# Expert tokens and results through row tables in DRAM, and expert weights in slices of 1024 columns

## The chip, the cores and the metric

The kernel runs on one core of one Trainium2 chip. The metric is the device time of one execution in microseconds, the median of several runs.
## The reference

Two decoder layers over 256 tokens of width 1024: an RG-LRU block and a dense SwiGLU, then forgetting attention and a mixture of eight SwiGLU experts of which each token uses two. The change is about the mixture:

```python
def _moe(xn, router, w_gu, w_down):
    logits = (xn @ router).astype(jnp.float32)
    top_v, top_i = lax.top_k(logits, TOP_K)              # TOP_K = 2
    w = jax.nn.softmax(top_v, axis=-1)
    gates = jnp.sum(w[..., None] * jax.nn.one_hot(top_i, N_EXPERTS, dtype=jnp.float32), axis=-2)
    y = jnp.zeros_like(xn)
    for e in range(N_EXPERTS):                           # 8 experts, D_EXP = 3584
        y = y + gates[..., e:e + 1].astype(xn.dtype) * _swiglu(xn, w_gu[e], w_down[e])
    return y
...
hn = _rmsnorm(x, norm_g[l, 1]); x = x + _moe(hn, ...);  return _rmsnorm(x, final_norm_g)
```

## The kernel before

All weights are float32 and stream once from DRAM in units of 1 MB (128 partitions x 2048 columns), 403 of them: 65 for the layers up to attention, 8 x 42 for the experts, and two that nobody uses. SyncE loads unit u into one of six slots of `raw` (L209) as soon as VectorE is done with unit u - 6 (`lo_done`). ScalarE copies it, rounded to float32r, into one of three slots of `w_hi` (L331, `split_hi`); it waits there until TensorE has used unit u - 3 (`unit_used`). VectorE puts the rest, raw - w_hi, into `w_lo` (L570, `split_lo`). TensorE multiplies in three parts (`mm3`, L959 to L961): hi x lo, lo x hi, hi x hi. ScalarE and VectorE run two units ahead of TensorE (LEAD = 2): with unit k on TensorE they split unit k + 2.

A loop over `jobs` passes of one expert each (eight, or sixteen where an expert has more than 128 tokens) holds for all engines. One pass is 42 units, cut in seven chunks of 512 hidden columns: four units of gate and up weights (`expert_in`, 512 columns each, so runs of 2 KB in DRAM), and two of down weights (`expert_out`). The token tiles `act_hi`, `act_lo` are the stationary operand of gate and up. After a chunk: silu of the gate on ScalarE (L544), product with up on VectorE (L925, `hid`), four transposes on TensorE (`hidden_T`, L1216), `hid_hi` on ScalarE (L548) and `hid_lo` on VectorE (L931). These stand ahead of the split of their place k in ScalarE's and VectorE's order. The hidden tiles are the stationary operand of `expert_out`.

The tokens of an expert come by TensorE: `gather` (L1179, L1180) multiplies the token rows with a 0/1 matrix `sel` that VectorE builds from the ranks of the router, 32 matmuls, between the second last and the last down unit of chunk 5. The results go back in the same way one pass later: at k = 0 ScalarE and VectorE split the result by the slots' gates (`y_hi` L528, `y_lo` L897), TensorE transposes the gated selection and multiplies (`scatter`, L1190, L1191, eight matmuls), VectorE adds to `x` (L905). After the loop comes the last scatter, then the final norm and the store.

What stands in what order is written out by hand for each engine; no planner is in it. Ahead of the loop come the router's small steps on VectorE, POOL's subtraction for the token rows' low part (L319), and filler matmuls (`keep_warm`, L994) that end with 14 just before the first expert.

## Time and profile before

| | |
|---|---|
| median of three runs (1528.9 to 1529.28) | 1529.24 us |
| span of the profiled execution | 1527.8 us |
| TensorE busy, share of the span | 1478.3 us, 97% |
| VectorE, ScalarE, POOL busy | 1177.1, 978.8, 20.4 us |
| DMA moved | 426.91 MB, mean 279 GB/s |
| DMA rate in the slices of the expert loop (38 us each) | 305 to 374 GB/s |
| matmuls of `expert_in` (each of L959 to L961) | 896 |
| expert loop, first to last matmul | about 503 to 1512.6 us |

A row of the order of time begins with the start and the duration in us; several instructions of one kind in a row are merged, with their number behind x; the idle time of the engine before it and what ended it stand in brackets. The duration of a matmul is longer than the distance to the next one, since they overlap: the distance of two starts is what one costs. "DMA share" is the mean busy share of the 16 DMA engines.

### The profile page before, as it was taken

The numbers are of one execution on the slowest core, as the hardware profiler recorded it, in microseconds if no ns is written. First come the engines' busy times: TensorE is split into PE (matmuls) and PEld (weight loads), VectorE is DVE, ScalarE is ACT, GpSimd is POOL, SyncE is SP. The second block draws the span as 40 slices with busy tenths as digits, with TensorE's granted clock in tenths as the row PEclk, the third lists the DMA queues.
The fourth block names the chain that finished last, engine by engine and source line by source line (L and its number), as shares of the span: only waits on it lengthen the run. The fifth ranks groups of instructions, "written<-read, shape, count | busy, mean of one in ns | idle before, by whom it ended". The sixth has DMA issues, their size and how long they took to land.

```text
span 1527.8 us, 20924 instructions
## 1 busy us (share of the span) xinstructions
PE 1478.3 (97%) x7697; PEld 1244.9 (81%) x7697; DVE 1177.1 (77%) x1030; ACT 978.8 (64%) x859; POOL 20.4 (1%) x30
## 2 busy tenths in 40 slices
PE   6979999999999999999999999999999999999996
PEld 5969999989777888788788878878878887887885
DVE  5765544484456888889898888888889888888887
ACT  4835344354343777777777777777776777777774
POOL 0200000000001000000000000000000000000000
PEclk8999999999999999999999999999999999999998
DMA  9444555645114699999999989989999999998993
GB/s 307 138 165 160 172 191 177 188 130 191 59 56 151 224 362 369 321 358 362 319 356 362 374 309 364 366 310 362 368 322 356 357 349 334 359 374 305 368 363 118
DMA packets 206372, 426.91 MB, mean 279 GB/s; under 512 B 8728, under 2 KB 51840, under 8 KB 206336
## 3 DMA queue, kind: packets, MB, share of 16 engines
q1 hardware_dynamic: 203552, 424.75, 78.4%
q10 hardware_dynamic: 2640, 1.15, 0.3%
q0 software_dynamic: 144, 0.52, 0.1%
q8 instruction: 23, 0.38, 0.1%
q14 instruction: 13, 0.11, 0.0%
HBM read 425.35 MB, written 1.05 MB: 279 GB/s over the span
## 4 chain that ended last, share of the span: by engine, by line
PE 91%; DVE 3%; ACT 3%; issue 2%; ACTq 1%; DMA 0%; POOL 0%; DVEq 0%; POOLq 0%; SPq 0%
PE bank L959 28%; PE bank L961 27%; PE bank L960 27%; PE bank L1216 2%; ACT w_hi L331 1%; DVE w_lo L570 1%; PE bank L1117 1%; PE bank L1180 1%; PE bank L1179 1%; ACT y_hi L528 1%; PE bank L1190 1%; PE bank L1191 1%; PE bank L1115 1%; PE bank L1140 0%; PE bank L1130 0%
## 5 line engine op out<-in xcount | busy, mean ns | idle before, releaser
L570 DVE TENSOR_TENSOR w_lo<-raw,w_hi 128x2048 fp32r<-128x2048 f32 x403 | 917.9, 2292 | 255.6 <-ACT w_hi L331 254.8
L331 ACT ACTIVATE w_hi<-raw 128x2048 fp32r<-128x2048 f32 x403 | 771.5, 1918 | 261.0 <-PE bank L961 251.0
L959 PE MATMUL bank<-w_hi,act_lo 128*128 128x512 f32 x896 | 355.1, 396 | 9.6 <-DVE w_lo L570 9.6
L961 PE MATMUL bank<-w_hi,act_hi 128*128 128x512 f32 x896 | 349.5, 390 | 0.0
L960 PE MATMUL bank<-w_lo,act_hi 128*128 128x512 f32 x896 | 349.2, 390 | 0.0
L959 PE MATMUL bank<-w_hi,hid_lo 128*128 128x512 f32 x536 | 213.3, 398 | 0.0
L960 PE MATMUL bank<-w_lo,hid_hi 128*128 128x512 f32 x536 | 212.4, 396 | 0.0
L961 PE MATMUL bank<-w_hi,hid_hi 128*128 128x512 f32 x536 | 212.3, 396 | 0.0
L959 PEld LDWEIGHTS bank<-w_hi,act_lo 128*128 128x128 f32 x896 | 168.3, 188 | 47.7 <-DVE w_lo L570 14.2
L961 PEld LDWEIGHTS bank<-w_hi,act_hi 128*128 128x128 f32 x896 | 168.2, 188 | 36.2
L960 PEld LDWEIGHTS bank<-w_lo,act_hi 128*128 128x128 f32 x896 | 168.5, 188 | 33.4
L959 PE MATMUL bank<-act_hi,w_lo 128*128 128x256 f32 x608 | 174.7, 287 | 11.2 <-DVE act_lo L587 11.2
L961 PE MATMUL bank<-act_hi,w_hi 128*128 128x256 f32 x608 | 173.2, 285 | 0.0
L960 PE MATMUL bank<-act_lo,w_hi 128*128 128x256 f32 x608 | 173.2, 285 | 0.0
L959 PEld LDWEIGHTS bank<-act_hi,w_lo 128*128 128x128 f32 x608 | 117.9, 194 | 13.5 <-issue 12.9
L961 PEld LDWEIGHTS bank<-w_hi,hid_hi 128*128 128x128 f32 x536 | 100.9, 188 | 24.4
L959 PEld LDWEIGHTS bank<-w_hi,hid_lo 128*128 128x128 f32 x536 | 101.0, 188 | 23.2
L960 PEld LDWEIGHTS bank<-w_lo,hid_hi 128*128 128x128 f32 x536 | 100.9, 188 | 23.2
L960 PEld LDWEIGHTS bank<-act_lo,w_hi 128*128 128x128 f32 x608 | 117.8, 194 | 0.5
L961 PEld LDWEIGHTS bank<-act_hi,w_hi 128*128 128x128 f32 x608 | 117.8, 194 | 0.0
L544 ACT ACTIVATE silu<-bank 128x512 f32<-128x512 f32 x56 | 33.5, 599 | 42.3 <-PE bank L961 42.2
L959 PE MATMUL bank<-w_hi,alt_lo 128*128 128x512 f32 x96 | 38.7, 403 | 6.2 <-DVE alt_lo L655 6.2
(226 smaller groups left out, 1158.9 us busy)
## 6 DMA issues: line engine op xcount, KB each, us to landing
raw<-in_moe_w_gu SPq DMA_DIRECT2D x226, 1024.0 KB, 6.6
raw<-in_moe_w_down SPq DMA_DIRECT2D x112, 1024.0 KB, 6.1
raw<-in_mlp_w_gu SPq DMA_DIRECT2D x22, 1024.0 KB, 5.0
raw<-in_mlp_w_down SPq DMA_DIRECT2D x11, 1024.0 KB, 5.0
raw<-in_lru_w_in SPq DMA_DIRECT2D x8, 1024.0 KB, 12.5
raw<-in_w_kvf SPq DMA_DIRECT2D x8, 1024.0 KB, 5.4
raw<-in_fox_w_qg SPq DMA_DIRECT2D x8, 1024.0 KB, 5.3
raw<-in_lru_w_out SPq DMA_DIRECT2D x4, 1024.0 KB, 5.2
```

What stands on the lines that cost most here:

```text
L331: a.activation(w_hi[:, u % SPL, :], raw[:, u % RAW, :], ACT.Copy).then_inc(hi_done, 1)
L528: a.activation(y_hi[:, HALF * half:HALF * half + HALF], bank[half][:], ACT.Copy, scale=gslot[:, 0:1]).then_inc(yhi_done, 1)
L544: a.activation(silu[:], bank[2][:], ACT.Silu).then_inc(e_silu, 1)
L570: v.tensor_tensor(w_lo[:, u % SPL, :], raw[:, u % RAW, :], w_hi[:, u % SPL, :].bitcast(f32), ALU.subtract).then_inc(lo_done, 1)
L959: t_.matmul(dst, l_lo, r_hi, start=start, stop=False)
L960: t_.matmul(dst, l_hi, r_lo, start=False, stop=False)
L961: return t_.matmul(dst, l_hi, r_hi, start=False, stop=stop)
L1115: t_.matmul(dst, c_sel[:, i % 2, queries], c_neg[:, keys], start=True, stop=False)
L1117: last = t_.matmul(dst, q_T[rows_h, hp, queries], k_T[rows_h, hp, keys], start=False, stop=True)
L1179: t_.matmul(dst, src_lo[:, w], sel[:, t, :], start=(t == 0), stop=False)
L1180: last = t_.matmul(dst, src_hi[:, w], sel[:, t, :], start=False, stop=(t == NT - 1))
L1216: last = t_.transpose(bank[4 + c % 2][:, n * P:(n + 1) * P], hid[:, n * P:(n + 1) * P], ident[:])
```

## The change

Tokens. The kernel gets two tables of 17 x 128 rows in DRAM, `tok_rows` and `y_rows`. POOL fills both with zeros, 17 DMAs of 0.5 MB each, behind its second and its third norm step. For each token two row numbers are worked out (`row_i`), one for each of its experts. POOL scales the normed token rows (`xs_g`) and writes them with four indirect DMAs to their rows. Expert 0 still takes its tokens by `gather`; each later one loads its 128 rows of `tok_rows` into `tok` in the pass before (an ACT DMA at k = 10), and TensorE transposes them (`tokens_T`, eight transposes after unit 37) into the token tiles. ScalarE doesn't enter the loop before all four writes have landed.

Results. There is no scatter. At the end of a pass ScalarE copies the 128 x 1024 result from PSUM to `y_sb` and issues its store to `y_rows`. After the loop POOL waits for all stores and issues four indirect gathers; VectorE multiplies each with the tokens' gates and adds it to `x`.

Weights. Gate and up are loaded in slices of 1024 columns (three pairs) and one of 512: units of [128, 2, 1024], runs of 4 KB. A pass is G0 U0 G1 D0 ... in the order of the tables `G_AT`, `U_AT`, `D_AT`. silu, `hid` and `hid_lo` work on 1024 columns, four times a pass instead of seven on 512; `hidden_T` stands after units 11, 23, 33 and 39. `expert_in` works on two PSUM banks in turn with the same stationary tile.

Place. A tile of 32 bytes (`pad_to_64_bytes`) is put ahead of the tiles that share one region. `hid_hi` starts at byte 174304 of a partition before and at 178560 afterwards, that is at 32 and at 0 past a multiple of 64; `hid_lo` likewise. `act_hi`, `act_lo`, `alt_hi`, `alt_lo` and the weight tiles start at a multiple of 64 in both.

```diff
-CH = D_EXP // 512
-JU = 6 * CH
+JU = 42
+NPAIR = 4
+WIDE = 1024
+G_AT, U_AT, D_AT = (0, 8, 20, 32), (4, 12, 24, 34), (16, 28, 36, 40)
+GU_UNITS, D_UNITS = (4, 4, 4, 2), (4, 4, 4, 2)
+T_AFTER = (11, 23, 33, 39)
+TOK_AFTER = 37
+ROWS = 17 * P
...
+        sb("pad_to_64_bytes", [P, PAD])
...
@@ sync @@
+                            kt, width = (2, WIDE) if n == 4 else (4, 512)
+                            lo = part + WIDE * p
+                            return e_gu[e][:, kt * (k - at):kt * (k - at) + kt, lo:lo + width], width
...
@@ gpsimd @@
             norm_scale(1)
+            pool.wait_ge(zeros_ready, 1)
+            for b in range(ROWS // P):
+                pool.dma_start(tok_rows[b * P:(b + 1) * P, :], zeros[:]).then_inc(tok_blank, 16)
             norm_scale(2)
+            for b in range(ROWS // P):
+                pool.dma_start(y_rows[b * P:(b + 1) * P, :], zeros[:]).then_inc(y_blank, 16)
...
+            for t in range(NT):
+                g.tensor_tensor(xs_g[:, t, :], xs[:, t, :], gmoe_bc[:], ALU.mult).then_inc(xsg_ready, 1)
...
+            for t in range(NT):
+                for c in range(2):
+                    g.indirect_dma_start(out=tok_rows[:, :], out_offset=bass.IndirectOffsetOnAxis(ap=row_i[:, c, t:t + 1], axis=0),
+                                         in_=xs_g[:, t, :], in_offset=None).then_inc(tok_sent, 16)
...
+            pool.wait_ge(y_stored, 16 * jobs + 1)
+            g.tensor_tensor(zeros[:, 0:2], neghalf[:], neghalf[:], ALU.add).then_inc(y_all_stored, 1)
+            pool.wait_ge(y_all_stored, 1)
+            for t in range(NT):
+                for c, into in enumerate((xs, xs_g)):
+                    g.indirect_dma_start(out=into[:, t, :], out_offset=None, in_=y_rows[:, :],
+                                         in_offset=bass.IndirectOffsetOnAxis(ap=row_i[:, c, t:t + 1], axis=0)).then_inc(y_back[t][c], 16)
...
@@ scalar @@
-            act.wait_ge(moe_blank, 2)
+            act.wait_ge(tok_sent, 4 * 16)
             act.wait_ge(njobs_ready, 1)
...
             with act.Fori(0, jobs) as j:
                 for k in range(JU):
+                    for p in range(NPAIR):
+                        if k == U_AT[p]:
+                            silu_pair(j, p, k)
+                    if k == 10:
+                        act.dma_start(tok[:], tok_rows[bass.ds(P * j + P, P), :]).then_inc(tok_loaded, 16)
                     split_hi(U_MOE + k + LEAD, J6 * j)
+                    for p in range(NPAIR):
+                        if k == T_AFTER[p] + 1:
+                            hid_hi_pair(j, p)
+                    if k == TOK_AFTER + 1:
+                        act.wait_ge(tok_T, j + 1)
+                        a.activation(act_hi[:, 0:4, :].rearrange("p c n -> p (c n)"), banks2[3][:], ACT.Copy).then_inc(tok_hi_done, 1)
+                act.wait_ge(unit_used, U_MOE + JU * j + JU)
+                act.wait_ge(y_stored, 16 * j + 1)
+                act.wait_ge(y_blank, 16 * (ROWS // P))
+                a.activation(y_sb[:], banks2[2][:], ACT.Copy).then_inc(y_free, 1)
+                act.wait_ge(y_free, j + 2)
+                act.dma_start(y_rows[bass.ds(P * j, P), :], y_sb[:]).then_inc(y_stored, 16)
...
@@ vector @@
                     split_lo(U_MOE + k + LEAD, J6 * j)
+                    for p in range(NPAIR):
+                        if k == T_AFTER[p] + 1:
+                            dve.wait_ge(e_hid_hi, NPAIR * j + p + 1)
+                            n = 256 * GU_UNITS[p]
+                            v.tensor_tensor(hid_lo[:]..., banks2[3][:, 0:n], hid_hi[:]..., ALU.subtract).then_inc(e_hid_lo, 1)
...
+            for t in range(NT):
+                for c, back in enumerate((xs, xs_g)):
+                    dve.wait_ge(y_back[t][c], 16)
+                    last = v.scalar_tensor_tensor(out=x[:, t, :], in0=back[:, t, :], scalar=gate_t[:, c, t:t + 1], in1=x[:, t, :],
+                                                  op0=ALU.mult, op1=ALU.add)
...
@@ tensor @@
+                for k in range(kt):
...
+                    for half in range(width // 512):
+                        w = slice(k * width + half * 512, k * width + half * 512 + 512)
+                        last = mm3(dst[half], act_hi[s], act_lo[s], w_hi[:, u % SPL, w], w_lo[:, u % SPL, w], kk == 0, kk == KD - 1)
...
+                        if k == D_AT[p]:
+                            pe.wait_ge(e_hid_lo, NPAIR * j + p + 1)
...
+                        if k == T_AFTER[p]:
+                            hidden_T(j, p)
+                    if k == TOK_AFTER:
+                        tokens_T(j)
```

On ScalarE at the end of a pass before, from the split of unit 40 on, `hid_hi` of the last chunk stands ahead of the split of unit 41; the eight `act_hi` copies are the next pass's tokens:

```order
L331 ACTIVATE w_hi<-raw 128x2048 [waits unit_used]
L547 REGISTER_ALU
L548 ACTIVATE hid_hi<-bank4 128x512 [waits e_T]
L330 REGISTER_ALU [waits raw_full4]
L331 ACTIVATE w_hi<-raw 128x2048 [waits unit_used]
L519 ISA
L520 ACTIVATE act_hi<-bank6,cols 128x128 [waits gathered]
```

And ScalarE at the end of a pass of the changed kernel, from the split of unit 42, the next expert's first, on:

```order
L381 ACTIVATE w_hi<-raw 128x2048 [waits unit_used]
L583 REGISTER_ALU
L585 ACTIVATE hid_hi<-bank6_7 128x512 [waits e_T]
L378 ISA
L380 REGISTER_ALU [waits raw_full0]
L381 ACTIVATE w_hi<-raw 128x2048 [waits unit_used]
L606 REGISTER_ALU
L607 ISA [waits unit_used]
L609 ACTIVATE y_sb<-bank4_5 128x1024 [waits y_blank,y_stored]
L610 REGISTER_ALU
L611 ISA [waits y_free]
L611 DMA y_rows<-y_sb 128x1024
```

`hid_hi` of the last pair has moved behind the split of unit 42, and the copy and the store of the result stand behind the split of unit 43.

TensorE at the same place of the changed kernel, from the last matmul of unit 39 to the first of unit 40 (the gather that stood between its like before is gone):

```order
L1020 MATMUL bank4_5<-w_hi,hid_hi 128x512
L1269 REGISTER_ALU
L1271 REGISTER_ALU [waits e_h]
L1275 MATMUL bank6_7<-ident,hid 128x128 [waits tok_lo_done]
L1275 MATMUL bank6_7<-ident,hid 128x128 x3
L1023 REGISTER_ALU [waits e_hid_lo]
L1018 MATMUL bank4_5<-w_hi,hid_lo 128x512 [waits lo_done]
```

The transposes of the last pair and the unit that waits for their `hid_lo` now stand directly behind each other.

## Rows read from the trace of the kernel before

**Rows 1.** Windows, busy us (instructions) per engine, clock, DMA share, GB/s:

```profile
160.00:200.00 40.00, 40.00 (x284) 37.49 (x283) 20.26 (x12) 15.41 (x11) 0.00 (x0) 1.00 0.55 180
...
1200.00:1400.00 200.00, 197.27 (x914) 162.02 (x913) 172.98 (x118) 149.31 (x113) 0.00 (x0) 1.00 0.95 346
```

**Rows 2.** Waits from 503 to 1513 us: us in total, times, longest:

```profile
ACT w_hi L331 <- PE bank L961: 204.0, 249, 2.7
...
PE bank L959 <- DVE w_lo L570: 9.6, 7, 1.4
```

**Rows 3.** Order of time on TensorE: attention's projection, expert_in, transposes, expert_out:

```profile
474.12 0.39 PE L959 MATMUL bank<-w_hi,alt_lo 128*128 128x512 f32 x1
...
476.39 0.39 PE L960 MATMUL bank<-w_lo,alt_hi 128*128 128x512 f32 x1
...
645.77 0.39 PE L960 MATMUL bank<-w_lo,act_hi 128*128 128x512 f32 x1
...
648.03 0.39 PE L961 MATMUL bank<-w_hi,act_hi 128*128 128x512 f32 x1
...
648.99 0.40 PE L960 MATMUL bank<-w_lo,act_hi 128*128 128x512 f32 x1
...
655.14 0.39 PE L959 MATMUL bank<-w_hi,hid_lo 128*128 128x512 f32 x1
...
659.82 0.40 PE L961 MATMUL bank<-w_hi,hid_hi 128*128 128x512 f32 x1
```

**Rows 4.** Order of time after the last matmul of the loop, ScalarE and VectorE:

```profile
1512.68 1.26 ACT L528 ACTIVATE y_hi<-bank,gslot 128x512 fp32r<-128x512 f32 x2 [0.97 <-PE bank L961]
1519.75 1.06 ACT L334 ACTIVATE xs<-x 128x1024 f32<-128x1024 f32 x1 [5.80 <-DVE x L905]
...
1522.18 2.48 DVE L949 SCALAR_TENSOR_TENSOR xs<-x,rstd,gfin_bc 128x1024 f32<-128x1024 f32 x2 [1.19 <-POOL rstd L304]
```

**Rows 5.** Order of time on TensorE ahead of the first expert:

```profile
496.82 0.36 PE L1179 MATMUL bank<-sel,alt_lo 128*128 128x128 f32 x1
...
500.49 3.24 PE L994 MATMUL bank<-ones 128*128 128x256 f32 x14
503.37 0.59 PE L959 MATMUL bank<-w_hi,act_lo 128*128 128x512 f32 x1
```

**Rows 6.** Order of time of all engines at a turn of the loop:

```profile
754.92 1.28 ACT L528 ACT_TABLE_LOAD   x1 [0.95 <-PE bank L961]
...
757.37 3.71 ACT L331 ACTIVATE w_hi<-raw 128x2048 fp32r<-128x2048 f32 x2
...
761.66 0.50 PE L959 MATMUL bank<-w_hi,act_lo 128*128 128x512 f32 x1 [1.37 <-DVE w_lo L570]
```

**Rows 7.** Groups of instructions by line and shape, 600 to 1500 us:

```profile
L931 DVE TENSOR_TENSOR hid_lo<-bank,hid_hi 128x512 fp32r<-128x512 f32 x50 | 34.2, 683 | 0.0
```

**Rows 8.** Windows around three gaps of TensorE, columns as in rows 1:

```profile
311.00:314.00 3.00, 2.74 (x14) 2.20 (x13) 1.20 (x4) 2.07 (x6) 0.00 (x0) 0.50 0.00 0
...
633.00:636.00 3.00, 1.63 (x8) 1.04 (x7) 2.98 (x2) 2.98 (x2) 0.00 (x0) 1.00 0.56 217
...
1515.70:1519.10 3.40, 3.29 (x8) 2.00 (x7) 2.13 (x4) 0.00 (x0) 0.00 (x0) 0.50 0.00 0
```

**Rows 9.** Order of time on TensorE ahead of attention:

```profile
310.13 3.04 PE L1001 MATMUL bank<-ident,xs 128*128 128x128 f32 x16 [1.96 <-DVE xs L580]
```

**Rows 10.** Order of time on POOL ahead of the first expert:

```profile
482.70 0.96 POOL L316 DMA_DIRECT2D gfin_bc<-in_final_norm_g  x1
486.25 4.57 POOL L319 TENSOR_TENSOR alt_lo<-xs,alt_hi 128x2048 fp32r<-128x2048 f32 x1 [2.58 <-ACT alt_hi L509]
```

**Rows 11.** DMA issues: engine, times, KB each, us to landing:

```profile
raw<-in_mlp_w_gu SPq DMA_DIRECT2D x22, 1024.0 KB, 5.0
...
out<-xs SPq DMA_DIRECT2D x2, 512.0 KB, 2.7
gfin_bc<-in_final_norm_g POOLq DMA_DIRECT2D x1, 512.0 KB, 4.5
```

More of the change, by code:

```diff
@@ L621, in _ @@
             dve.wait_ge(consts, 5)
+            for e in range(NE):
+                v.memset(first_row[:, :, e:e + 1], float(P * e))
             v.tensor_copy(ident_bf[:], ident[:]).then_inc(consts_v, 1)
@@ L831, in _ @@
             norm_lo(4, R_NORM + 3 * KD, act_hi, act_lo)
-            LOG, GT, EQ, MASK, INC, EXP, GATE, OFF = range(8)
+            LOG, GT, EQ, MASK, INC, EXP, GATE, OFF, SPILL, SLOT = range(10)
             both = lambda n: route[:, n, :, :]
@@ L916, in _ @@
                 for k in range(JU):
-                    if k == 0:
-                        y_lo_part(j)
-                    if k == 4 or (k >= 8 and k % 6 == 2 and k // 6 < CH):
-                        c = 0 if k == 4 else k // 6
-                        dve.wait_ge(e_silu, CH * j + c + 1)
-                        dve.wait_ge(unit_used, U_MOE + JU * j + k)
-                        if c:
-                            dve.wait_ge(e_T, CH * j + c)
-                        v.tensor_tensor(hid[:], silu[:], bank[3][:], ALU.mult).then_inc(e_h, 1)
@@ new lines, in _ @@
+                    split_lo(U_MOE + k + LEAD, J6 * j)
+                    for p in range(NPAIR):
+                        if k == T_AFTER[p] + 1:
+                            dve.wait_ge(e_hid_hi, NPAIR * j + p + 1)
+                            n = 256 * GU_UNITS[p]
+                            v.tensor_tensor(hid_lo[:].rearrange("p b n -> p (b n)")[:, 0:n], banks2[3][:, 0:n],
+                                            hid_hi[:].rearrange("p b n -> p (b n)")[:, 0:n].bitcast(f32), ALU.subtract).then_inc(e_hid_lo, 1)
@@ L1182, in gather @@
                         last.then_inc(gathered, 1)
-            def scatter(j):
-                pe.wait_ge(ylo_done, 2 * j + 2)
-                for half in range(2):
-                    w = slice(HALF * half, HALF * half + HALF)
-                    for t in range(NT):
-                        dst = bank[4 + 2 * half + t][:]
-                        t_.matmul(dst, sel_T[:, t * P:(t + 1) * P], y_lo[:, w], start=True, stop=False)
-                        t_.matmul(dst, sel_T[:, t * P:(t + 1) * P], y_hi[:, w], start=False, stop=True).then_inc(scattered, 1)
@@ L1211, in expert_out, with hidden_T @@
                 last.then_inc(unit_used, 1)
-            def hidden_T(j, c):
-                pe.wait_ge(e_h, CH * j + c + 1)
-                for n in range(4):
-                    last = t_.transpose(bank[4 + c % 2][:, n * P:(n + 1) * P], hid[:, n * P:(n + 1) * P], ident[:])
-                last.then_inc(e_T, 1)
+            def hidden_T(j, p):
+                pe.wait_ge(e_h, NPAIR * j + p + 1)
+                if p == NPAIR - 1:
+                    pe.wait_ge(tok_lo_done, KD + j + 1)
+                elif p:
+                    pe.wait_ge(e_hid_lo, NPAIR * j + p)
+                for n in range(2 * GU_UNITS[p]):
+                    last = t_.transpose(banks2[3][:, n * P:(n + 1) * P], hid[:, n * P:(n + 1) * P], ident[:])
+                last.then_inc(e_T, 1)
@@ L1219, in _, with tokens_T @@
+            def tokens_T(j):
+                pe.wait_ge(tok_loaded, 16 * j + 16)
+                pe.wait_ge(e_hid_lo, NPAIR * j + NPAIR - 1)
+                for n in range(KD):
+                    last = t_.transpose(banks2[3][:, n * P:(n + 1) * P], tok[:, n * P:(n + 1) * P], ident[:])
+                last.then_inc(tok_T, 1)
             pe.wait_ge(src_ready, 1)
```

270 lines of the change are left out of this document (126 added, 144 removed).

## The prediction

> **What bounds the kernel now.** I read the stretches of the windows view first, then the waits, then the order of time around one expert, and last the two ends of the expert loop. In the expert loop TensorE is busy 197 of 200 us, at the full granted clock, while the DMA engines are 95% busy at 346 GB/s [rows 1]. Two resources are nearly full, so the waits must say which one is late. ScalarE waits 204 us for TensorE and nothing in the loop waits for a DMA; TensorE itself waits only 9.6 us, in seven waits of about 1.4 us, all for the VectorE half of a weight split [rows 2]. So TensorE sets the pace, and what is worth something is TensorE work taken out of the loop, or a TensorE wait put in.
>
> The pitch of TensorE shows what its work costs. With the token tiles as stationary operand ten steps take 648.03 - 645.77 = 2.26 us, 0.227 each; with the hidden tiles twenty steps take 4.68 us, 0.234 each [rows 3]. A weight unit (1 MB, 12 matmuls) thus lasts 2.72 us, or 2.81 us with the hidden tiles. One expert lasts 126.1 us: ScalarE takes up the last result at 1512.68 [rows 4], some 0.3 after the place where a next matmul would start, and the loop's first matmul starts at 503.37 [rows 5]; eight experts in 1009.0. Check: 28 x 2.72 + 14 x 2.81 = 115.5; 28 transposes at 0.127 (four lengthen the run from 648.03 to 648.99 by 0.96 - 2 x 0.227 = 0.51) = 3.6; a gather of 32 matmuls 500.49 - 496.82 = 3.7 [rows 5]; a scatter of 8 at 0.23 = 1.85; two selection transposes 0.2; the wait 1.4. Sum 126.3, which is near enough.
>
> **The change part by part.**
>
> *Taken out per expert:* gather 3.7, scatter 1.85, selection transposes 0.2, together -5.7 us on TensorE. *Added:* eight token transposes at 0.127, +1.0. The 28 hidden transposes stay, in four groups instead of seven.
>
> *The wait after the last transposes, added.* ScalarE and VectorE now do hid_hi and hid_lo of the last pair behind the split of unit 42 (the next expert's first), and that split needs the slot of unit 39, which TensorE has just used when it starts the transposes. TensorE's next instruction, unit 40, needs hid_lo. In the old order the gather and one more unit (3.7 + 2.8 us) lay over this chain; now nothing does. Its length: from the start of a split on ScalarE to the TensorE unit that needs it is 761.66 - 757.37 = 4.3 us [rows 6], then hid_lo of 512 columns, 0.68 less 0.1 of overlap [rows 7], plus about 0.2 until ScalarE is woken: 5.1. The four transposes fill 0.4. TensorE stands 4.7 us per expert. Queued behind it are units 40 and 41; who waits for those is the copy of y.
>
> *The turn of the loop.* Today ScalarE loads its table (754.92), writes y_hi, splits (757.37), and TensorE goes on at 761.66 after 1.4 us of waiting [rows 6]. The table load stays, at the loop's first split. The two y_hi copies (1.2) go; a copy of 1024 columns comes (0.69 of y_hi's 512, two in 1.26 with their overlap [rows 4], and 0.4 for 512 more, by the 1.86 of a split's 2048 [rows 6]: 1.1), then a semaphore to itself, a DMA issue (0.4, an estimate between nothing and the 0.96 of POOL's issue, below) and the branch, which stood in idle time before: some +1.9 against -1.2. The wait grows by 0.7, seven times.
>
> *Wider silu, hid and hid_lo (1024 columns instead of 512).* They stand between splits. At unit 4 the chain is 0.2 + 1.0 + 4.3 = 5.5 against two units of TensorE, 5.44; at the others the transposes give 1 us more. I take 0.2 per expert, up to 1.
>
> *The hidden tiles' place.* They start 32 bytes past a multiple of 64 now and on a multiple of 64 afterwards, where all token tiles stand. If the place is what costs 0.007 per matmul, 168 matmuls per expert gain 1.2 us, and the dense layers' 264 gain 1.85 in all. The other explanation is that consecutive groups keep the same stationary tile and change bank. I take the place (rival 1 says why).
>
> The Trainium skill, "SBUF — State Buffer", section Door 1: The DMA port swizzle, speaks of lines of 16 bytes; both addresses begin such a line, so by it the shift gives nothing, and the sum below would be 11 us higher. No row of the kernel before can tell which holds.
>
> *Sum per expert:* -5.7 + 1.0 + 4.7 + 0.2 - 1.2 = -1.0, and +0.7 at each of seven turns: 8 x -1.0 + 7 x 0.7 = -3.1 us; dense layers -1.85.
>
> *The clock.* The seven waits of 1.4 us left it at 1.00 (the stretch from 633 [rows 8]). But after a gap of 1.96 us, before 310.13 [rows 9], it stood at 0.50, and again for 3.4 us in the last scatter, after the last wait [rows 8]. That is 1.2 instead of 2.4 GHz. A gap of 4.5 us is far past that. A stretch of 3.4 us at half speed costs 1.7 us of TensorE work, right where units 40 and 41 stand, which wait for nothing else; two such stretches would cost 3.4. I take 2.0 per expert, +16; bounds 0 and +27.
>
> *Weights in 1024-column slices.* DMA rows of 4 KB instead of 2 KB for 24 of 28 gate and up units. Nothing waits for a load today, so a faster load is worth nothing [rows 2]. The token and y transfers add 1 MB to 44 per expert, at the forecast period 353 GB/s, within the 305 to 374 that slices of the loop show.
>
> *Zeroing the row tables.* 34 DMAs of 0.5 MB on POOL's queue, behind its second and third norm step, the next of which comes 170 us or more later. In the dense layers the DMA is 55% busy at 180 GB/s [rows 1], a unit of 1.05 MB each 5.8 us; a load is issued five units (29 us) before its split and lands in 5 [rows 11], so it has 24 us in hand. 17 zero blocks at the 340 GB/s of the loop take 26 us, in which weights still get a share. I put it at 0; if they got none, 2 to 10 us.
>
> *Before the loop.* POOL must multiply 2 x 1024 columns after its subtraction (4.57 us for 2048 columns, ending 490.8 [rows 10]): 495.4, at twice that price 500. The rows are known about 497, where the gather that needs the same ranks starts now [rows 5]. Then four indirect DMAs. No row shows one; the nearest is POOL's broadcast, 0.96 us to issue [rows 10] and 4.5 to land [rows 11]. The last lands at 504.3, or 509 with dearer issues. Only then may ScalarE enter the loop: value load 0.8 (estimate), table load and split and VectorE 5.6, so unit 2 is ready at 511, or 516. TensorE starts at 503.4 as now, since its filler matmuls set that [rows 5], and wants it at 508.8. +3 (1 to 7), and +1 for the clock.
>
> *After the loop.* Now 1512.68 to 1527.8, 15.1 us [rows 4]. Afterwards: copy 1.0, issue and store to DRAM 2.7 as the output's [rows 11], POOL's token addition 0.3, first gather landed 4.5, then four additions on VectorE of 1.25 each (the final products: 2.48 for two [rows 4]): 5.0, the gathers coming 0.96 apart beside them. That is 13.8 with the handoffs. From the squares at 1519.75 the end is unchanged, 8.1. Together 21.9: +6.8, bounds +4 (gathers landing in 2.7) and +11 (2 us to issue each).
>
> **Sum.** 1527.8 - 3.1 - 1.85 + 16 + 4 + 6.8 = 1549.7 us of span. The median of the runs, 1529.2, lies 1.4 above the profiled span: 1551.1.
>
> **Rivals.**
> 1. *The hidden matmuls stay at 0.234.* For it: the rows allow it, and the page's rule above. 1551.1 + 11.3 = 1562.4. Against: in the output projection the groups change bank too, and with aligned tiles ten steps take 476.39 - 474.12 = 2.27 us, 0.227 each [rows 3].
> 2. *Bank change with the same stationary tile is what costs.* Then the gate and up matmuls, which now do this too, also go to 0.234: 336 x 0.007 x 8 = 19 more than rival 1, 1581.
> 3. *The clock holds.* Place: units 40 and 41 after the 4.7 us wait. The 1.4 us waits held it, the 1.96 us one lost it; it decides whether a long wait inside dense work counts as the sparse work around 310 did. Without it and its 1 at the start: 1534.1. This is the case not slower: with the two ends at their lower bounds (-2, -2.8) it gives 1529.3, and faster needs one more such gain.
> 4. *DMA becomes the bound.* If the engines can't hold more than the 346 GB/s of today [rows 1], 45.1 MB take 130.3 us, 2.5 more than the 127.8 (126.1 - 1.0 + 0.7 + 2.0) forecast: 1571. Against it: ScalarE never waited for a load, and slices at up to 374 GB/s stand in the page. The Trainium skill, "HBM Reference", section Specifications, gives 358 GB/s per core; by that the expert would need 126 us, no bound here.
>
> That the change does not do what it says (more than eight passes) I exclude: the 896 token matmuls are eight passes of 112, set by the router's counts.
>
> **How the numbers follow.** Forecast 0.50; rival 1 0.20; rival 2 0.06; rival 3 0.15; rival 4 0.04; faster for a reason I do not see 0.05. The range reaches from rival 3 with one end a little cheaper to rival 1 with the ends dearer and to rival 4: 1533 to 1571; outside it lie rival 2, the lower part of rival 3 and the unseen, 0.17 in all. A measurement of this kernel tells 0.2% (3 us) from no change. Faster 0.05, same 0.07 (half of rival 3), slower 0.88.
>
> **What would show it.** In the changed kernel: a TensorE wait of 4 to 5 us for hid_lo eight times; after each a granted clock of 0.5; hidden matmuls at a pitch of 0.227; a wait of about 2 us at the turn; POOL's four scatters before ScalarE's first split in the loop; 20 to 24 us from the last matmul to the end. It would be wrong if the clock holds through the long waits, or if an indirect DMA costs several times the broadcast.

## The result, and the profile after

| | before | after |
|---|---|---|
| median | 1529.26 us | 1595.23 us (1590.66 to 1598.34, four runs) |
| ratio | | 1.0436, 95% interval 1.0413 to 1.0458 |
| span of the profiled execution | 1527.8 | 1590.9 |
| start of the loop's first matmul | 503.4 | 506.0 |
| last matmul of the last expert, end | 1512.6 | 1567.3 |
| from there to the end | 15.2 | 23.6 |
| one expert | 126.1 | 133.15 (from the first long wait to the second 130.7) |

The direction was forecast, the size was not: 66 us slower instead of 22, and outside the range of 1533 to 1571. Of the 63 us of span, 52 lie in the expert loop, 8.4 behind it and 2.6 ahead of it.

Busy time, the clock and the DMA rate in 40 slices of the changed kernel:

```profile
PE 1467.7 (92%) x7417; PEld 1226.2 (77%) x7417; DVE 1128.7 (71%) x840; ACT 957.1 (60%) x745; POOL 53.6 (3%) x78
...
PEclk8999999999999999999899899999989989999996
...
GB/s 309 143 204 339 185 185 185 231 313 132 54 146 110 378 367 335 324 372 369 258 375 365 279 362 364 331 309 376 362 261 386 357 275 362 366 347 294 372 337 92
```

TensorE is busy 10.6 us less than before although the loop is 52 us longer: it waits, and part of its busy time is at half the clock. The waits from 503 to 1567 us (us in total, times, longest), beside [rows 2]:

```profile
ACT w_hi L381 <- PE bank L1020: 276.1, 232, 8.1
...
PE bank L1018 <- DVE hid_lo L989: 41.9, 16, 4.6
PE bank L1018 <- DVE w_lo L629: 25.8, 32, 2.4
```

Where TensorE had seven waits of 1.4 us, it now has 32 for `w_lo` of up to 2.4 us and 16 for `hid_lo`, eight of them 4.6 us long. Below, "place k" is the point of a pass at which TensorE comes to unit k of it, and what a wait costs is the distance from the last matmul ahead of it to the next one, less the usual 0.227 us. ScalarE still waits for TensorE and nothing in the loop waits for a load. The place of the long wait, in the order of time on TensorE, ScalarE and VectorE:

```profile
888.05 0.60 PE L1275 MATMUL bank<-ident,hid 128*128 128x128 f32 x4
888.25 1.91 ACT L381 ACTIVATE w_hi<-raw 128x2048 fp32r<-128x2048 f32 x1 [0.80 <-PE bank L1020]
...
890.07 0.58 ACT L585 ACTIVATE hid_hi<-bank 128x512 fp32r<-128x512 f32 x1
890.19 2.29 DVE L629 TENSOR_TENSOR w_lo<-raw,w_hi 128x2048 fp32r<-128x2048 f32 x1 [0.42 <-ACT w_hi L381]
892.40 0.68 DVE L989 TENSOR_TENSOR hid_lo<-bank,hid_hi 128x512 fp32r<-128x512 f32 x1
...
893.22 0.79 PE L1018 MATMUL bank<-w_hi,hid_lo 128*128 128x512 f32 x1 [4.57 <-DVE hid_lo L989]
...
893.80 0.63 PE L1019 MATMUL bank<-w_lo,hid_hi 128*128 128x512 f32 x1
894.23 0.63 PE L1020 MATMUL bank<-w_hi,hid_hi 128*128 128x512 f32 x1
```

This is the chain that the prediction drew: the split of unit 42, `hid_hi`, `w_lo`, `hid_lo`, with nothing over it. The pitch behind it is 0.43 us instead of 0.227. The windows behind this wait, behind the turn of the loop, and of a long stretch (columns as in [rows 1]):

```profile
893.50:898.50 5.00, 5.00 (x13) 3.83 (x13) 0.00 (x0) 0.00 (x0) 0.00 (x0) 0.50 0.69 269
899.50:905.00 5.50, 5.50 (x26) 4.56 (x25) 2.29 (x1) 3.34 (x3) 0.00 (x0) 1.00 0.24 71
909.50:912.50 3.00, 3.00 (x7) 2.40 (x8) 3.00 (x2) 1.14 (x1) 0.00 (x0) 0.50 0.60 176
...
1200.00:1400.00 200.00, 190.88 (x842) 154.79 (x841) 161.43 (x79) 138.81 (x82) 0.00 (x0) 0.97 0.94 349
```

The clock falls to 1.2 GHz twice in most passes: for 6.8 us around the end of the long wait (3.4 us in the first pass) and for 3.4 us behind the turn (six of the seven). At half the clock a matmul lasts 0.427 us, 0.2 more than at the full one. The turn and two of the smaller waits:

```profile
901.79 1.03 ACT L609 ACTIVATE y_sb<-bank 128x1024 f32<-128x1024 f32 x1 [1.15 <-PE bank L1020]
902.98 0.35 ACTq L611 DMA_DIRECT2D y_rows<-y_sb  x1
903.83 1.28 ACT L381 ACT_TABLE_LOAD   x1 [1.01 <-issue]
905.13 5.51 ACT L381 ACTIVATE w_hi<-raw 128x2048 fp32r<-128x2048 f32 x3
...
909.42 0.79 PE L1018 MATMUL bank<-w_hi,act_lo 128*128 128x512 f32 x1 [2.36 <-DVE w_lo L629]
...
948.58 0.50 PE L1018 MATMUL bank<-w_hi,act_lo 128*128 128x512 f32 x1 [0.32 <-DVE w_lo L629]
...
1009.29 0.49 PE L1018 MATMUL bank<-w_hi,hid_lo 128*128 128x512 f32 x1 [0.67 <-DVE hid_lo L989]
```

**One expert of 133.15 us, counted in the trace.** 504 matmuls at 0.2267 are 114.3 and 36 transposes at 0.127 are 4.6, together 118.9. The rest is lost: 4.7 in the long wait, 2.8 in the 13 matmuls at half the clock behind it (13 x 0.2, and 0.16 at the first), 2.5 at the turn and 1.5 in the seven slow matmuls behind that, 1.7 in three waits at places 6, 15 and 27 (some 0.6 each, as at 948.58, with the matmul behind it), 0.9 at place 36 (the row of 1009.29), and 0.3 in smaller ones. Sum 133.3.

### The profile page after: what moved, and what is told of

It is laid out like the page before. It is cut to its first block, busy times and chain, and to the rows that moved or that the text cites. A ratio compares the mean times of both kernels' runs of the same rounds, so it can differ in the third digit from the quotient of the medians.

```text
span 1590.9 us, 19935 instructions
## 1 busy us (share of the span) xinstructions
PE 1467.7 (92%) x7417; PEld 1226.2 (77%) x7417; DVE 1128.7 (71%) x840; ACT 957.1 (60%) x745; POOL 53.6 (3%) x78
## 4 chain that ended last, share of the span: by engine, by line
PE 70%; DVE 10%; ACT 9%; issue 8%; ACTq 1%; DMA 1%; POOL 0%; DVEq 0%; POOLq 0%; SPq 0%
PE bank L1018 22%; PE bank L1020 21%; PE bank L1019 21%; DVE w_lo L629 6%; ACT w_hi L381 6%; DVE hid_lo L989 2%; PE bank L1275 1%; PE bank L1176 1%; ACT silu L579 1%; PE bank L1174 1%; ACT y_sb L609 1%; PE bank L1199 0%; PE bank L1283 0%; ACT L579 0%; PE bank L1189 0%
## 5 line engine op out<-in xcount | busy, mean ns | idle before, releaser
L1018 PE MATMUL bank<-w_hi,act_lo 128*128 128x512 f32 x896 | 361.4, 403 | 25.8 <-DVE w_lo L629 25.8
L1018 PE MATMUL bank<-w_hi,hid_lo 128*128 128x512 f32 x536 | 220.4, 411 | 41.9 <-DVE hid_lo L989 41.9
L1019 PE MATMUL bank<-w_lo,hid_hi 128*128 128x512 f32 x536 | 216.4, 404 | 0.0
L1020 PE MATMUL bank<-w_hi,hid_hi 128*128 128x512 f32 x536 | 216.1, 403 | 0.0
L1018 PEld LDWEIGHTS bank<-w_hi,hid_lo 128*128 128x128 f32 x536 | 105.7, 197 | 68.7 <-DVE w_lo L629 38.4
L1020 PEld LDWEIGHTS bank<-w_hi,hid_hi 128*128 128x128 f32 x536 | 105.2, 196 | 23.4
L1019 PEld LDWEIGHTS bank<-w_lo,hid_hi 128*128 128x128 f32 x536 | 106.1, 198 | 21.5
L579 ACT ACTIVATE silu<-bank 128x1024 f32<-128x1024 f32 (+1 forms) x32 | 29.5, 922 | 43.0 <-PE bank L1020 42.9
## 6 DMA issues: line engine op xcount, KB each, us to landing
y_rows<-zeros POOLq DMA_DIRECT2D x17, 512.0 KB, 10.6
```

Of the source, the lines that this page charges most:

```text
L579: a.activation(silu[:, 0:n], banks2[0][:, 0:n], ACT.Silu).then_inc(e_silu, 1)
L1018: t_.matmul(dst, l_lo, r_hi, start=start, stop=False)
L1019: t_.matmul(dst, l_hi, r_lo, start=False, stop=False)
L1020: return t_.matmul(dst, l_hi, r_hi, start=False, stop=stop)
```

## The experiments

The theory after this count: TensorE's time in the loop is its matmuls, plus waits that stand in ScalarE's and VectorE's order at four kinds of places, plus the slow clock behind the long ones. Its rivals: the DMA would be the next bound at once; the clock falls for another reason than the standing engine; and, on the pitch, the hidden tiles' place does nothing. All times are medians. The runs of the kernel before beside them gave 1528.7 to 1529.1.

### e1_cover: units laid over the chain

```diff
-T_AFTER = (11, 23, 33, 39)
-TOK_AFTER = 37
+T_AFTER = (11, 23, 33, 37)
+TOK_AFTER = 39
...
@@ tensor, at the end of a pass @@
+                pe.wait_ge(tok_lo_done, KD + j + 1)
```

> The changed kernel with two steps exchanged: the last pair's transposes stand after unit 37 instead of 39 (their hid_hi goes to the half of the hidden tile that units 36 and 37 have used), the token transposes after unit 39 instead of 37. Theory A: the 4.6 us TensorE wait before unit 40 is the chain split of unit 42, hid_hi, hid_lo with nothing over it, and the 13 matmuls at half the clock behind it come from that wait alone. Then hid_lo comes behind the split of unit 40, with units 38 and 39 (5.4 us) over 5.1 us of chain: per expert 4.7 of wait and 13 x 0.2 + 0.2 = 2.8 of clock go, 8 x 7.5 = 60, from 1595 to about 1535 us, a period of 125.7. Rival B, the DMA is the bound behind it: 45.1 MB per expert at no more than the 346 to 350 GB/s of the kernel before give a period of 129 to 130, 1565 us, with ScalarE waiting for raw. Rival C, the wait moves to the token tiles: their act_hi and act_lo (1.0 + 1.2 us) now stand behind the split of unit 42; if that chain is longer than units 40 and 41, TensorE stands 1 to 3 us before the next expert's first unit, and the time is 1545 to 1575.

Measured: 1533.49 us, ratio to before 1.0031 (1.0019 to 1.0042). Of the 62 us less than the changed kernel, 60 were forecast. The waits of e1_cover from 503 to 1508 us:

```profile
ACT w_hi L381 <- PE bank L1020: 217.8, 232, 3.4
...
PE bank L1018 <- DVE w_lo L629: 25.2, 31, 2.4
...
PE bank L1018 <- DVE hid_lo L989: 5.3, 8, 0.7
```

The long wait for `hid_lo` is gone in all eight passes (the eight of 0.7 us that are left are those at place 36), ScalarE waits for no load, and the token tiles come in time. So the long wait and what hangs on it are worth 7.7 us per expert, and the DMA is no bound at a period of 125.6. The turn is as it was, gaps of 2.32 to 2.43 us, but only five of these seven are followed by a slow stretch. The changed kernel spent 71.7 us at half the clock in its loop, e1_cover 17.1.

### e2_fill and e2b_fill9: the wait kept, the clock held

```diff
                         if k == T_AFTER[p]:
                             hidden_T(j, p)
+                            if p == NPAIR - 1:
+                                keep_warm(9, 0)          # 19 in e2_fill
```

> The changed kernel with 19 filler matmuls (128 x 256, 0.21 us each) on a bank that is free, behind the last transposes of each expert; they fill some 4.05 of the 4.6 us that TensorE stands before unit 40. The result is untouched. Theory A, the fall of the clock comes from the standing engine: the wait for hid_lo ends at the same moment, but the 13 matmuls behind it run at 0.227 instead of 0.427 us; 8 x 2.8 = 22 us less, about 1573, and the granted clock stays at 1.00 there. If instead the clock falls for another reason (the load of DMA, VectorE and ScalarE together, say), the time stays at 1595 and 0.50 stands behind the fillers too.

Measured: 1596.92 us, which looks like the second answer and isn't. The fillers were too long:

```profile
893.66 8.37 PE L1053 MATMUL bank<-ones 128*128 128x256 f32 x38
901.67 0.58 PE L1018 MATMUL bank<-w_hi,hid_lo 128*128 128x512 f32 x1
```

A filler on plain float32 operands is recorded as two matmuls, so 19 made 8.2 us, and unit 40 started 8.45 us behind the transposes (893.22 to 901.67) instead of 5.17: 3.3 per expert, 26 in all. What they cost the clock gave back. With nine:

> As e2_fill with 9 filler matmuls instead of 19. In e2_fill each filler was recorded as two matmuls of 0.216 us, so that 19 lasted 8.2 us, 4 longer than the wait that they were to fill; at the full clock 9 last 3.9. Theory A (the standing engine makes the clock fall): hid_lo ends as in the changed kernel, the 13 matmuls behind it run at 0.227; 8 x 2.8 = 22 less than 1595, about 1573, and somewhat less where the shorter slow stretch lets the turn's 2.4 us wait hold the clock too. Theory B (it falls for another reason): 1595 still.

Measured: 1570.48 us, 24.8 less than the changed kernel. `hid_lo` ends as late after the transposes as before (5.0 us), and behind it:

```profile
885.69 0.60 PE L1275 MATMUL bank<-ident,hid 128*128 128x128 f32 x4
886.12 4.05 PE L1053 MATMUL bank<-ones 128*128 128x256 f32 x18
890.86 0.49 PE L1018 MATMUL bank<-w_hi,hid_lo 128*128 128x512 f32 x1 [0.68 <-DVE hid_lo L989]
```

```profile
891.00:896.00 5.00, 5.00 (x23) 4.12 (x24) 0.15 (x1) 1.92 (x1) 0.00 (x0) 1.00 0.69 271
```

The second fence is a window: 23 matmuls in 5 us at a clock of 1.00, with a DMA share of 0.69 as in the changed kernel and VectorE (0.15 us busy) and ScalarE (1.92) nearly as idle. So at this place it is TensorE's standing that takes the clock, and of the 7.7 us that e1_cover gained per expert about 3 are clock and 4.7 wait.

### e3_pad_only and e3b_pad160: the kernel before with the tiles moved

```diff
         gslot = sb("gslot", [P, 1])
+        sb("pad_to_64_bytes", [P, 8])         # [P, 40] in e3b_pad160
```

> The kernel before with nothing but a tile of 32 bytes ahead of the shared region, so that hid_hi and hid_lo start on a multiple of 64 bytes. Theory A, the place of the hidden tiles is what costs 0.007 us per matmul: their pitch goes from 0.234 to 0.227, 8 x 168 x 0.007 + 264 x 0.007 = 11.3, about 1518 us. Rival: the pitch in the changed kernel has another cause (the order of units, tiles of 1024 columns, the two banks in turn); then nothing changes and the time stays at 1529.

Measured: 1527.71 us, ratio 0.9994 (0.9985 to 1.0004): no change. A multiple of 64 bytes is not what counts. But the pitch had moved a little, to 0.232, and larger multiples were left to compare: `hid_hi` starts 224 past a multiple of 256 in the kernel before, at 0 in e3_pad_only and at 128 in the changed kernel, and `act_hi`, `act_lo` and `alt_hi` start at 128 too.

> The kernel before with a tile of 160 bytes ahead of the shared region instead of 32: hid_hi starts at byte 174464, which is 128 past a multiple of 256, as it is in the changed kernel (178560) and as act_hi, act_lo and alt_hi are; in e3_pad_only it stood at a multiple of 256 and the pitch was 0.232. Theory A (the place counts, but by 256 bytes and not by 64): pitch 0.227, about 11 us less than 1529, 1518. Theory B (the place counts by something larger, or relative to another tile): the pitch stays between 0.230 and 0.234 and the time at 1527 to 1529.

Measured: 1519.14 us, ratio 0.9942 (0.9926 to 0.9959). Twenty steps of `expert_out` in e3_pad_only (the first two rows), in the changed kernel (the next two) and in e3b_pad160:

```profile
654.36 0.39 PE L962 MATMUL bank<-w_hi,hid_hi 128*128 128x512 f32 x1
...
659.00 0.39 PE L961 MATMUL bank<-w_lo,hid_hi 128*128 128x512 f32 x1
```

```profile
1010.09 0.39 PE L1018 MATMUL bank<-w_hi,hid_lo 128*128 128x512 f32 x1
...
1014.62 0.39 PE L1020 MATMUL bank<-w_hi,hid_hi 128*128 128x512 f32 x1
```

```profile
525.10 0.39 PE L960 MATMUL bank<-w_hi,hid_lo 128*128 128x512 f32 x1
...
529.64 0.39 PE L962 MATMUL bank<-w_hi,hid_hi 128*128 128x512 f32 x1
```

They last 4.64, 4.53 and 4.54 us, where [rows 3] has 4.68: 0.232, 0.227 and 0.227. The gain, 9.5 us on the kernel before, comes from where the tiles lie and from nothing else, and is had by 160 bytes of padding. Why 128 past a multiple of 256 is good, and whether it is the hidden tiles alone, isn't shown: the pad moves all tiles of the shared region. The rule of the Trainium skill that the prediction weighed ("SBUF — State Buffer", section Door 1: The DMA port swizzle), lines of 16 bytes, would have had no gain here, since the hidden tiles start on such a line in all four kernels. The measurement differs from it: the pitch goes from 0.234 to 0.227.

### e4_result_late: the result out of the turn

```diff
-                act.wait_ge(unit_used, U_MOE + JU * j + JU)
-                ...
-                a.activation(y_sb[:], banks2[2][:], ACT.Copy).then_inc(y_free, 1)
-                act.wait_ge(y_free, j + 2)
-                act.dma_start(y_rows[bass.ds(P * j, P), :], y_sb[:]).then_inc(y_stored, 16)
+                    if k == 7:
+                        result_out(j)                    # the same steps for the pass before
+            result_out(jobs)
```

> The changed kernel with the copy of the result y and its store moved from the end of a pass to place 7 of the next one (both row tables get one block more, rows shifted by 128; the last copy stands behind the loop). Theory A: the turn's wait of 2.4 us is copy, DMA issue, branch and table load ahead of ScalarE's first split, and the 7 matmuls at half the clock behind it come from its length. Left at the turn is table load 1.3, split 1.9, VectorE 2.3 and 0.3 of handoff, 5.8 us, against two units of 5.4: a wait of about 0.4 to 1, which holds the clock as the 1.4 us of the kernel before did. Saved 7 x (1.7 + 1.5) = 22 us, about 1573. Rival: the table load and the branch are what it costs, not the copy; then the wait stays above 2 and the time at 1590 or more.

Measured: 1562.86 us, 32 less than the changed kernel, 10 more than forecast. ScalarE at the turn:

```profile
1020.00 1.92 ACT L381 ACTIVATE w_hi<-raw 128x2048 fp32r<-128x2048 f32 x1 [7.82 <-PE bank L1027]
1021.94 1.28 ACT L381 ACT_TABLE_LOAD   x1
1023.23 1.92 ACT L381 ACTIVATE w_hi<-raw 128x2048 fp32r<-128x2048 f32 x1
```

Without the copy ScalarE comes to the table load before TensorE is done with unit 41, and TensorE no longer waits at the turn at all, where a wait of 0.4 to 1 us had been expected; behind unit 2 of the first pass the eight long waits are the only ones above 0.7 us. So the copy, its wait for unit 41 and its store were the turn's cost. The wait explains 7 x 2.5 = 17.5; the rest is the clock. The same gaps of 4.57 us are now followed by 6.8 us at half speed in five passes and by 3.4 us in three; 44.4 us in all against 71.7, and 27.3 x (1 - 0.227 / 0.427) = 12.8. Together that is 30.3, and the two profiled executions are 30.0 apart.

### e5_earlier_T: the wide steps apart

```diff
-T_AFTER = (11, 23, 33, 39)
+T_AFTER = (9, 21, 31, 39)
```

> The changed kernel with the first three groups of transposes two units earlier (after units 9, 21, 31 instead of 11, 23, 33), so that hid_hi and hid_lo of 1024 columns no longer stand in the same two units as silu or just ahead of the down unit that needs them. Theory A: the waits for w_lo of 0.6 us at places 15 and 27 and the one of 0.9 us for hid_lo at place 36 are these wide steps between the splits; they go, the 0.6 at place 6 (table load, silu) stays: 8 x 2.1 = 17 us less than 1595, about 1578. Rival: the wide steps delay the splits wherever they stand, and waits of the same size appear two units earlier: no change.

Measured: 1571.32 us, 24 less. Over its loop:

```profile
PE bank L1018 <- DVE hid_lo L989: 36.5, 8, 4.6
PE bank L1018 <- DVE w_lo L629: 20.9, 16, 2.5
```

Eight waits for `hid_lo` instead of 16 and 16 for `w_lo` instead of 32: those at places 15, 27 and 36 are gone and none has come elsewhere, only the one at place 6 and the turn remain. The 7 us more than the 17 of the waits are in part the clock (only three of the seven turns are followed by a slow stretch, which is worth some 3), the rest is no more than the spread of the changed kernel's runs, 1590.7 to 1598.3; the two profiled executions are 21.6 apart.

### e7_all: all repairs together

This is e1_cover, e4_result_late and e5_earlier_T in one, `T_AFTER = (9, 21, 31, 37)`, with `act.wait_ge(tok_sent, 4 * 16)` moved from ahead of the loop to place 10.

> All repairs in one: the transposes after units 9, 21, 31 and 37, the token transposes after 39, the result's copy and store at place 7 of the next pass, and ScalarE's wait for the four row writes only ahead of the first load that needs them. Left per expert are 504 matmuls at 0.227 and 36 transposes at 0.127, 119 us, and 0.6 at place 6. If TensorE alone bounds: from e1_cover (1533.5) 7 x 3.6 for the turn, 8 x 2.1 for the wide steps and 1.7 at the start go, about 1490. That needs 45.1 MB in 119.6 us, 377 GB/s, where the loop of e1_cover shows a mean of about 360 and slices up to 392. Rival (the DMA becomes the bound): at 365 GB/s 123.6 us per expert, about 1520, with ScalarE waiting for raw <- DMA.

Measured: 1488.91 us, ratio 0.9745 (0.9729 to 0.9761), where 1490 was forecast. A window of it, and the one kind of wait of TensorE's that is left in the loop, at place 6 of each pass:

```profile
900.00:1100.00 200.00, 199.65 (x910) 164.49 (x909) 175.32 (x87) 150.74 (x90) 0.00 (x0) 1.00 1.00 379
```

```profile
1120.20 0.50 PE L1024 MATMUL bank<-w_hi,act_lo 128*128 128x512 f32 x1 [0.32 <-DVE w_lo L635]
```

DMA share 1.00 at 379 GB/s, and still no wait for a load: a share of 1.00 is not yet the bound, for each load is issued early, and the one with the least in hand (its split starts at 901.70) landed 2.0 us ahead. The 358 GB/s of the Trainium skill ("HBM Reference", section Specifications), which the prediction held against rival 4, are by the same section a core's share while both cores of its pair stream, and a core alone measures above it. The trace agrees: this kernel runs on one core and moved 379.

### e8_halves4k and e8_runs2k: the width of the slices

```diff
-                sp.dma_start(dst, src).then_inc(raw_full[u % RAW], 16)
...
+                if width == WIDE and not down:           # e8_runs2k only: halves by columns, runs of 2 KB
+                    parts = [(slice(0, kt), slice(h, h + 512)) for h in (0, 512)]
+                else:                                    # both: halves by row blocks, runs as they were
+                    parts = [(slice(h, h + kt // 2), slice(0, width)) for h in (0, kt // 2)]
+                for ks, ns in parts:
+                    sp.dma_start(dst[:, ks, ns], src[:, ks, ns]).then_inc(raw_full[u % RAW], 16)
```

> Control for e8_runs2k: e7_all with every weight unit loaded by two DMAs of 512 KB, its first and its second half of the row blocks, so that the runs in DRAM keep their length (4 KB for the wide units). Both theories: as e7_all, 1489 us, since nothing waits for a load; a few us more if the doubled issues on SyncE (0.8 us each) delay the loads.

> e7_all with every weight unit loaded by two DMAs of 512 KB, and the gate and up units of 1024 columns halved by columns, so that their runs are 2 KB again as in the kernel before. Theory A: the width of the slices is worth nothing to the time. Back-to-back a unit lands 2.70 us behind the one ahead in the kernel before and 2.56 in e7_all; 24 x 0.14 = 3.4 us of DMA time per expert on top of 42 x 2.56 + 2.6 = 110 is still under the period of 119.9. So the same as e8_halves4k within 2 us. Rival: the DMA engines are 99 to 100% busy in e7_all's loop, so their time is the bound, and 3.4 us per expert come out in full: 27 us more than e8_halves4k, with ScalarE waiting for raw <- DMA.

Measured: 1488.23 and 1489.04 us, ratios 0.9738 (0.9722 to 0.9755) and 0.9738 (0.9722 to 0.9754). The window of e8_runs2k (DMA share and rate at its end):

```profile
900.00:1100.00 200.00, 199.65 (x911) 164.64 (x910) 175.89 (x88) 150.15 (x90) 0.00 (x0) 1.00 1.02 381
```

Runs of 2 KB instead of 4 cost nothing, even at this rate. The third part of the change, the wide slices, is worth nothing in its DMA rows.

### e9_start: POOL out of VectorE's way

```diff
             pool.wait_ge(gmoe_loaded, 16)
+            pool.wait_ge(rows_ready, 1)
             for t in range(NT):
                 g.tensor_tensor(xs_g[:, t, :], xs[:, t, :], gmoe_bc[:], ALU.mult).then_inc(xsg_ready, 1)
```

> e7_all with POOL's two multiplications for the token rows (4.65 us) behind the wait for the row numbers instead of ahead of it. Theory A: they run beside VectorE's small router steps and stretch two of them (1.14 and 2.31 us for what lasts 0.16 otherwise), which makes the 3.3 us gap of TensorE before the rank matmuls, and the 6.8 us at half the clock behind it. Now the row writes end some 4.6 us later, at about 511, which nobody misses before the load at place 10 (530). Saved 3.3 of gap and 0.5 to 1.5 of clock: 1484 to 1485. Rival: the gap is the router chain itself, lengthened by the row numbers; then 1489 stays.

Measured: 1483.59 us, 5.3 less than e7_all. In the changed kernel POOL multiplied from 487.11 to 491.7, and two of VectorE's steps beside it were

```profile
488.33 1.14 DVE L906 TENSOR_SCALAR rcol<-top 128x2 f32<-128x2 f32 x1
...
489.47 2.31 DVE L908 TENSOR_TENSOR route<-route,top 128x16 f32<-128x16 f32 x1
```

and in e9_start the same two were

```profile
490.78 0.17 DVE L913 TENSOR_SCALAR rcol<-top 128x2 f32<-128x2 f32 x1
...
490.94 0.17 DVE L915 TENSOR_TENSOR route<-route,top 128x16 f32<-128x16 f32 x1
```

The other small steps in that stretch kept their length (0.16 to 0.24 us) in both. TensorE's gap of 3.3 us before the rank matmuls is gone, and from 493 to 499.5 us the granted clock is 1.00 where the changed kernel has 0.50.

### e10_table: one table for copies and silu

```diff
             with act.Fori(0, jobs) as j:
+                a.activation(warm[:, 2:4], neghalf[:], ACT.Silu)
                 for k in range(JU):
```

(`warm` is the padding tile, given a name; it stands on e9_start.)

> e9_start with a silu of 2 columns at the head of each pass on ScalarE, so that the table that the turn loads is silu's and the copies run under it; the second table load (1.28 us, ahead of the first silu) goes. Theory A: the wait of 0.6 us at place 6 is that table load standing between unit 3 and the split of unit 6; 8 x 0.6 = 4.8 less than e9_start, about 1480. Rival: the load is hidden (silu of 1024 columns and the split alone make the wait), or the copies load their own table again; then no change or a loss of 8 x 1.3.

Measured: 1476.82 us, ratio 0.9662 (0.9646 to 0.9678): 6.8 less than e9_start, 2 more than the 4.8 forecast. In the profiled executions a pass lasts 118.90 us instead of 119.48, 4.7 in all; another 2.3 lie ahead of 480 us, where both kernels issue the same steps, so they are not the change's. ScalarE's table loads in the loop of e9_start (the first two rows) and of e10_table (the third; the first of both stands ahead of 503 us):

```profile
L580 ACT ACT_TABLE_LOAD x8 | 10.3, 1283 | 0.1
L382 ACT ACT_TABLE_LOAD x7 | 9.0, 1283 | 0.1
```

```profile
L602 ACT ACT_TABLE_LOAD x7 | 9.0, 1283 | 0.1
```

The copies load none of their own. A window of e10_table:

```profile
900.00:1100.00 200.00, 199.97 (x913) 165.20 (x912) 175.56 (x88) 150.40 (x91) 0.00 (x0) 1.00 1.00 378
```

TensorE is busy 199.97 of 200 us. This version beats both kernels, the one before by 52 us and the changed one by 118. Of the 52, the place of the tiles gives 9.5 to the kernel before as well (e3b_pad160). What the tables alone are worth isn't shown, for the kernel before was never run with its own waits repaired.

## Why the prediction was wrong in size

The mechanisms were the right ones in the main; three terms of the sum were too small: the clock, the wide steps and the start.

**What held.** TensorE bounds, and nothing waits for a load. The gather, scatter and transposes came out at the prices given: 504 matmuls and 36 transposes in 118.9 us. The long wait was named with its chain and its length (4.7 forecast, 4.7 measured). The hidden matmuls run at 0.227 and the token ones too, so rivals 1 and 2 fall; rival 3 falls in the first long wait and rival 4 in e7_all. That the hidden matmuls came out at 0.227 was luck all the same: the prediction put it down to a multiple of 64, which e3_pad_only shows to be worth nothing, and the tiles happened to come to lie 128 past a multiple of 256. The zero blocks cost nothing: the gaps of TensorE that end at 111.2, 307.0 and 480.0 us stand within 0.1 us of the same times in e3b_pad160, which has no zero blocks.

**The clock, +14 us.** "I take 2.0 per expert" is the first term that was mis-sized. It rested on one stretch of 3.4 us at half speed [rows 8] and counted only the long wait. The stretch behind the long wait is 6.8 us, of which some 1.1 lie in the wait itself, and costs 2.8; and the turn's wait, grown from 1.4 to 2.4 us, loses the clock as well in six of seven turns and costs 1.5. The prediction noted that a gap of 1.4 held the clock and one of 1.96 lost it, and sized the turn's new wait at 2.1; it did not put the two together. That makes 4.3 per expert, 30 us over the loop (the first long wait had only 3.4 us behind it, and one of the seven turns kept the clock), where 16 were taken. The upper bound of 27 was too low too.

**The wide steps, +19 us.** "I take 0.2 per expert, up to 1" measured 2.6. The chain was drawn at unit 4 alone, 5.5 us against two units of 5.44, and came out 0.6 too long there, because the table load stood in it: ScalarE's silu had to wait for it (e10_table took it out). For the others the prediction said that "the transposes give 1 us more". But `hid_hi` and `hid_lo` of 1024 columns stand in the same two units as silu, 1.0 on ScalarE and 1.2 on VectorE; at place 36 it is the chain of the long wait once more (a split, `hid_hi`, `w_lo`, `hid_lo`), now with two units over it and still 0.9 too long. e5_earlier_T shows all three gone by moving one table of numbers.

**The turn, +3 us.** 2.1 forecast, a gap of 2.4 measured, 2.5 with the first matmul's delay. The steps were the right ones: copy, issue and branch took 2.04 (901.79 to 903.83) where 1.9 was put, and ScalarE's wait for the last matmul ahead of them is 1.15, where it was 0.95 [rows 6].

**The ends.** Ahead of the loop +4 was forecast. From the gap at 478.4, 3.7 us earlier than in the kernel before, to the first matmul at 506.0, and with the 2.0 us that TensorE loses at unit 2 (a gap of 1.8), it is 8.3. The prediction had POOL's multiplication late for the row writes and didn't ask what runs beside it: VectorE's two small steps (e9_start). The 0.8 put for ScalarE's value load is shown by no row: from its last `act_hi` copy to the table load it is 3.2 us in the changed kernel, the wait for the row writes in it, and 0.14 in e7_all, which has the value load there but not that wait. The 3.7 us ahead of 478 are not all the place's, of which 1.85 was forecast: 1.6 lie ahead of 111 us, where the kernel before had 3.4 us more at half the clock; 1.6 in the dense layers from there to 307, where the place was to work; and 0.5 behind, where the kernel before lost the clock at 310 and the changed one did not. Behind the loop 23.6 against 21.9. The gathers:

```profile
1571.79 0.99 POOL L369 DMA_INDIRECT xs<-y_rows,row_i  x1 [0.27 <-POOL zeros L365]
...
1576.16 1.28 DVE L998 SCALAR_TENSOR_TENSOR x<-xs,gate_t,x 128x1024 f32<-128x1024 f32 x1 [7.50 <-DMA xs<-y_rows,row_i]
1578.92 1.28 DVE L998 SCALAR_TENSOR_TENSOR x<-xs_g,gate_t,x 128x1024 f32<-128x1024 f32 x1 [1.48 <-DMA xs_g<-y_rows,row_i]
```

An indirect DMA takes 1.0 us of POOL, and the first gather lands 4.3 us after its issue, so the broadcast of [rows 10, 11] was a good neighbour for it. But the issues come 1.27 apart, not 0.96, and the other three gathers land 5.7 us after theirs. So VectorE waits 1.48 us for the second, and that is the error here: the sum had the later gathers come beside the additions.

**The sum again with what was measured:** 1549.7 + 14 (clock) + 19 (wide steps) + 3 (turn) + 4.3 (start) - 1.85 (ahead of 478) + 1.7 (end) = 1589.9, against a span of 1590.9.

## What to carry to other kernels

An exchange that saves TensorE work is paid by the order of the engines beside it: with splits two units ahead, every step put between two splits has 5.4 us of cover, and each place has to be counted by itself, not the likeliest one and the rest by analogy. Once a wait has passed the length that the trace shows to be harmless, add the slow clock behind it to its price, for each such place. And before a change is given up for being slow, look where its steps stand: with the tables in DRAM the kernel was 4.4% slower in the first order of steps and is 3.4% faster in the last, with the table load of e10_table and the 0.6% of the tiles' place among it.

## What the runs showed of the hardware that was not expected

- The pitch of the 128x512 matmuls on the hidden tiles changed with where these start within 256 bytes: 0.234 us at 224, 0.232 at 0, 0.227 at 128 past a multiple. Three places were measured, and other tiles moved with them. 160 bytes of padding are worth 0.6% of the kernel before.
- Gaps of TensorE and the clock, over the fourteen profiled executions: those of 1.3 to 1.8 us at the turn, at unit 2 and ahead of the router held it; the one of 1.97 at 305 us lost it in three (the kernel before, e3_pad_only, e10_table) and held it in eleven; those of 2.32 to 2.52 at the turn lost it in 21 of 35 (six of seven in the changed kernel, three of seven in e5_earlier_T); those of 4.57 lost it in 24 of 24, for 3.4 or for 6.8 us. So the same gap in the same code can cost 1.5 or 2.8 us, and this moves a kernel by some ten microseconds: e4_result_late gained 15 more than the waits it took away.
- A gap is not the only thing that loses the clock: in e2_fill, e8_runs2k and e9_start it stood at 0.50 for 3.4 us from 385 us on, behind attention's small matmuls and with no wait of TensorE in the 25 us ahead. Why there, isn't shown.
- Two tiny VectorE steps of 0.17 us lasted 1.14 and 2.31 us beside POOL's multiplications of 128x1024; others beside them kept their length.
- DMA engines at a share of 1.00 and 378 to 381 GB/s kept nobody waiting, with runs of 4 KB and of 2 KB alike.
- ScalarE's copies run under silu's table without loading their own: one load of 1.28 us per pass in e10_table, two in e9_start.
- The first of four indirect gathers of 128 rows landed 4.3 us after its issue, the other three 5.7 us after theirs.
